# Splitting a weight slot in two halves: a four-layer transformer stack on one core

## The reference, cut to what matters

```python
def second_block(x, c, ada_w, ...):            # layers 3 and 4; layers 1 and 2 are built alike
    c_act = jax.nn.silu(c)
    for l in range(DEPTH):
        mod = (c_act @ ada_w[l] + ada_b[l])[:, None, :]
        sh_m, sc_m, gt_m, sh_f, sc_f, gt_f = jnp.split(mod, 6, axis=-1)
        h = rms_norm_2(x, norm_mix[l]) * (1 + sc_m) + sh_m
        y = hybrid_mixer(h, ...) if l % 2 == 0 else retention_mixer(h, ...)
        x = x + gt_m * y
        h = rms_norm_2(x, norm_ffn[l]) * (1 + sc_f) + sh_f
        x = x + gt_f * swiglu(h, ffn_w_in[l], ffn_w_out[l])
    return x
```

## Time and profile before

| | |
|---|---|
| median of 3 runs | 1724.1 us (1721.39 to 1725.34) |
| the profiled execution | 1721.6 us, span 1719.8 us |
| mean granted TensorE clock | 0.921 of full speed |
| TensorE matmuls busy | 1539.8 us, 90% of the span |
| VectorE, ScalarE, GpSimd busy | 1064.8, 719.7, 281.2 us |
| idle time of TensorE, total | 180 us |
| HBM read | 333.8 MB, 195 GB/s over the span |

### The profile page before, as it was taken

How to read it: one execution, slowest core, us unless ns; L and a number is a source line. 1 busy time by engine, 2 the same in 40 slices (tenths; PEclk the granted TensorE clock), 3 DMA queues, 4 the chain that set the end, 5 groups by cost and what they waited for, 6 DMA issues and landing times. The chain is left out here.

```text
span 1719.8 us, 27368 instructions
## 1 busy us (share of the span) xinstructions
PE 1539.8 (90%) x11950; PEld 1495.1 (87%) x11950; DVE 1064.8 (62%) x1278; ACT 719.7 (42%) x803; POOL 281.2 (16%) x221
## 2 busy tenths in 40 slices
PE   2888689999798779999999787999999998999999
PEld 2887579999788679999899686999999996989998
DVE  6776568688545447778675654667547763455544
ACT  2533345533553344543377432443334443343332
POOL 0000101044000012024200112000126900300012
PEclk7998579999799778999899997899999999989999
DMA  9660258888342045988544001477645772436560
GB/s 396 239 247 24 109 219 314 338 300 325 114 154 98 13 159 183 338 308 322 220 148 172 25 1 68 169 300 274 244 172 221 272 275 90 172 123 240 202 220 26
DMA packets 47207, 336.64 MB, mean 196 GB/s; under 512 B 5360, under 2 KB 5744, under 8 KB 6768
## 3 DMA queue, kind: packets, MB, share of 16 engines
q1 hardware_dynamic: 46224, 333.03, 51.9%
q10 hardware_dynamic: 864, 1.87, 0.3%
HBM read 333.83 MB, written 1.05 MB: 195 GB/s over the span
## 5 line engine op out<-in xcount | busy, mean ns | idle before, releaser
L420 DVE TENSOR_TENSOR weights_hi_lo<-ring,weights_hi_lo 128x2048 fp32r<-128x2048 f32 x213 | 512.2, 2406 | 397.5 <-ACT weights_hi_lo L414 396.3
L414 ACT ACTIVATE weights_hi_lo<-ring 128x2048 fp32r<-128x2048 f32 x213 | 407.6, 1915 | 630.0 <-PE PS L522 345.6
L522 PE MATMUL PS<-hi,weights_hi_lo 128*128 128x256 f32 x3200 | 526.9, 288 | 26.0 <-DVE weights_hi_lo L420 17.6
L522 PEld LDWEIGHTS PS<-hi,weights_hi_lo 128*128 128x128 f32 x3200 | 451.5, 196 | 29.8 <-DVE weights_hi_lo L420 19.5
L792 PE MATMUL PS<-acts_hi_lo,weights_hi_lo 128*128 128x256 f32 x3552 | 438.6, 286 | 29.4 <-DVE weights_hi_lo L420 16.3
L792 PEld LDWEIGHTS PS<-acts_hi_lo,weights_hi_lo 128*128 128x128 f32 x3552 | 432.3, 193 | 36.0 <-DVE weights_hi_lo L420 19.9
L522 PE MATMUL PS<-lo,weights_hi_lo 128*128 128x256 f32 x1600 | 327.0, 286 | 0.0
L522 PEld LDWEIGHTS PS<-lo,weights_hi_lo 128*128 128x128 f32 x1600 | 253.7, 195 | 0.0
L431 DVE CUSTOM_DVE_ANT_0 ring<-ring,cond 128x1024 f32<-128x1024 f32 x192 | 247.0, 1325 | 1.0 <-DMA smallS<-in_small_dram 0.9
L740 POOL CAST acts_hi_lo<-arena 128x512 fp32r<-128x512 f32 x74 | 67.1, 907 | 977.8 <-PE PS L792 544.7
L522 PE MATMUL PS<-weights_hi_lo,hi 128*128 128x256 f32 x1248 | 204.4, 286 | 10.1 <-DVE weights_hi_lo L420 8.9
(11 more groups left out here) (339 smaller groups left out, 1091.4 us busy)
## 6 DMA issues: line engine op xcount, KB each, us to landing
ring<-in_stream_dram SPq DMA_DIRECT2D x313, 1024.0 KB, 4.9
constS<-in_const_dram SPq DMA_DIRECT2D x1, 1856.0 KB, 11.4
cond<-in_rows_dram SPq DMA_DIRECT2D x2, 512.0 KB, 5.9
arena<-in_x_dram ACTq DMA_DIRECT2D x1, 1024.0 KB, 12.5
smallS<-in_small_dram SPq DMA_DIRECT2D x1, 883.0 KB, 12.7
out_dram<-arena ACTq DMA_DIRECT2D x2, 256.0 KB, 2.4
out_dram<-arena SPq DMA_DIRECT2D x2, 256.0 KB, 2.8
constS<-in_const_dram SPq DMA_DIRECT2D x1, 320.0 KB, 13.5
```

The source lines that it names most:

```text
L414: act.activation(wsp[:, g % 2, 0, :], ring[:, n % RING, :], ACT.Copy).then_inc(*hi_ready.one())
L420: dve.tensor_tensor(wsp[:, g % 2, 1, :], ring[:, n % RING, :], wsp[:, g % 2, 0, :].bitcast(F32), ALU.subtract).then_inc(used["dve"], 1)
L522: mm = pe.matmul(o, lhs, rhs, start=k + g + j == 0, stop=k == KD - 1 and j == 2, skip_group_check=True)
```

## The change

1. `split_hi`, `split_lo`: each slot is split by two operations of 1024 columns. The first half of a buffer may be written when TensorE has finished the first half of slot g - 2 (new semaphore `half_multiplied`), the second as before. VectorE signals the first half by `half_lo_ready`, the second by `used["dve"]`.
2. Column products wait for the first half before k = 0 and for the second before k = 4.
3. Row products go over all k with g = 0 and then over all k with g = 1, waiting for the second half of weights and activations in between; the last slot keeps the old order and waits for both halves first. `split_acts` works on one tile at a time and waits for one tile at a time (`state["mixed"]` now has an entry for each).
4. The norm's parts on ScalarE and VectorE are in two functions each, squares and root, and scaling. In `start_phase` ScalarE does squares and root ahead of the first slot's split, and VectorE the reciprocal ahead of its last modulation slot. ScalarE issues positions, constants and small inputs before it waits for the condition row.

```diff
 CW = SLOT // KD
+HALF = SLOT // 2
...
         multiplied, hi_ready = sig("slot_multiplied"), sig("hi_ready")
+        half_multiplied, half_hi_ready, half_lo_ready = sig("half_slot_multiplied"), sig("half_hi_ready"), sig("half_lo_ready")
         acts_hi, acts_lo = sig("acts_hi_ready"), sig("acts_lo_ready")
         def close():
...
             g = product_no[n]
-            if g >= 2:
-
-                act.wait_ge(multiplied.sem, g - 1)
-            act.activation(wsp[:, g % 2, 0, :], ring[:, n % RING, :], ACT.Copy).then_inc(*hi_ready.one())
+            for half, at, released, ready in ((0, 0, half_multiplied, half_hi_ready), (1, HALF, multiplied, hi_ready)):
+                if g >= 2:
+
+                    act.wait_ge(released.sem, g - 1)
+                act.activation(wsp[:, g % 2, 0, at:at + HALF], ring[:, n % RING, at:at + HALF], ACT.Copy).then_inc(*ready.one())
         def split_lo(dve, n):
             g = product_no[n]
-            dve.wait_ge(hi_ready.sem, g + 1)
-            dve.tensor_tensor(wsp[:, g % 2, 1, :], ring[:, n % RING, :], wsp[:, g % 2, 0, :].bitcast(F32),
-                              ALU.subtract).then_inc(used["dve"], 1)
+            for half, at, ready, done in ((0, 0, half_hi_ready, (half_lo_ready.sem, 1)), (1, HALF, hi_ready, (used["dve"], 1))):
+                dve.wait_ge(ready.sem, g + 1)
+                dve.tensor_tensor(wsp[:, g % 2, 1, at:at + HALF], ring[:, n % RING, at:at + HALF],
+                                  wsp[:, g % 2, 0, at:at + HALF].bitcast(F32), ALU.subtract).then_inc(*done)
         def mod_sums(dve, order, n, q, kk):
...
             def _(pe):
...
                 for i, n in enumerate(gemm):
-
-                    pe.wait_ge(used["dve"], ordinal[n][1])
                     if i >= banks:
...
                     for k in range(KD):
+                        if k == 0:
+                            pe.wait_ge(half_lo_ready.sem, product_no[n] + 1)
+                        if k == KD // 2:
+                            mm.then_inc(*half_multiplied.one())
+                            pe.wait_ge(used["dve"], ordinal[n][1])
                         for j, (w, h) in enumerate(pieces(w_hi, w_lo, hi, lo)):
...
-            def act_part(act):
+            def act_root(act):
                 for u, tiles in enumerate(UNITS):
...
                 act.activation(r, PS[:, 0, 0:TT], ACT.Sqrt, bias=cst("eps"), scale=1.0 / D).then_inc(*xrt.one())
+
+            def act_scale(act):
                 for k in range(KD):
...
-            def dve_part(dve):
+            def dve_root(dve):
                 dve.wait_ge(*xrt.at(1))
                 dve.reciprocal(r, r).then_inc(*xr.one())
+
+            def dve_scale(dve):
                 dve.wait_ge(*rx.at(1))
...
-            return pe_part, act_part, dve_part
+            return pe_part, (act_root, act_scale), (dve_root, dve_scale)
         def start_phase(blk):
...
             def _(act):
+                act.dma_start(posI[:, :], pos_in).then_inc(*inp.dma())
                 act.dma_start(constS[:, 0:EARLY_CONST], const[:, 0:EARLY_CONST]).then_inc(*inp.dma())
-                act.dma_start(posI[:, :], pos_in).then_inc(*inp.dma())
+                act.dma_start(smallS[:, 0:early_small], small[:, 0:early_small]).then_inc(*biases.dma())
                 act.wait_ge(*cond_in.at(16))
-                act.dma_start(smallS[:, 0:early_small], small[:, 0:early_small]).then_inc(*biases.dma())
                 act.dma_start(raw, x_in).then_inc(*x_in_sig.dma())
...
                         "p (k t) -> p k t", t=SEQ), ACT.Copy).then_inc(*xt.one())
+                norm[1][0](act)
                 for n in following:
                     split_hi(act, n)
-                norm[1](act)
+                norm[1][1](act)
...
             def _(pe):
...
                 dve.wait_ge(*biases.at(16))
-                for _, n, q, kk in todo:
+                for i, (_, n, q, kk) in enumerate(todo):
                     mod_sums(dve, order, n, q, kk)
+                    if i == len(todo) - 2:
+                        norm[2][0](dve)
                 for n in following:
                     split_lo(dve, n)
-                norm[2](dve)
+                norm[2][1](dve)
             close()
         def split_acts(pool, lhs, slots, before=0, ready=None):
...
                 a = rows_no[n]
-                if ready:
-                    pool.wait_ge(*ready[i])
-                if a >= 2:
-
-                    pool.wait_ge(multiplied.sem, product_no[rows_slots[a - 2]] + 1)
-                src = lhs[:, 2 * i:2 * i + 2, :]
-                pool.tensor_copy(asp[:, a % 2, 0, :, :], src).then_inc(*acts_hi.one())
-                pool.wait_ge(acts_hi.sem, a + 1)
-                pool.tensor_tensor(asp[:, a % 2, 1, :, :], src, asp[:, a % 2, 0, :, :].bitcast(F32),
-                                   ALU.subtract).then_inc(*acts_lo.one())
+                for g, released in enumerate((half_multiplied, multiplied)):
+                    if ready:
+                        pool.wait_ge(*ready[2 * i + g])
+                    if a >= 2:
+
+                        pool.wait_ge(released.sem, product_no[rows_slots[a - 2]] + 1)
+                    src = lhs[:, 2 * i + g, :]
+                    pool.tensor_copy(asp[:, a % 2, 0, g, :], src).then_inc(*acts_hi.one())
+                    pool.wait_ge(acts_hi.sem, 2 * a + g + 1)
+                    pool.tensor_tensor(asp[:, a % 2, 1, g, :], src, asp[:, a % 2, 0, g, :].bitcast(F32),
+                                       ALU.subtract).then_inc(*acts_lo.one())
         def rows_gemm_phase(blk, name, l, lhs, half, acts_split=0, acts_ready=None, next_norm=None):
...
             def _(pe):
                 for i, n in enumerate(slots):
-
-                    pe.wait_ge(used["dve"], ordinal[n][1])
                     w_hi, w_lo = halves_of(n, "rows")
                     a = rows_no[n]
-                    pe.wait_ge(acts_lo.sem, a + 1)
+                    pe.wait_ge(acts_lo.sem, 2 * a + (2 if i == last else 1))
                     a_hi, a_lo = asp[:, a % 2, 0, :, :], asp[:, a % 2, 1, :, :]
-                    for k in range(KD):
-                        if before and i == 0 and k == KD - 1:
+                    pe.wait_ge(half_lo_ready.sem, product_no[n] + 1)
+                    if i == last:
+
+                        pe.wait_ge(used["dve"], ordinal[n][1])
+                    for g, k in sorted(((g, k) for g in range(2) for k in range(KD)), key=lambda o: o[::-1] if i == last else o):
+                        if before and i + g == 0 and k == KD - 1:
...
                                 pe.wait_ge(*t)
-                        for g in range(2):
-                            for j, (w, x) in enumerate(pieces(w_hi, w_lo, a_hi, a_lo)):
-                                mm = pe.matmul(y_of(k), w[:, g, k * P:(k + 1) * P], x[:, g, :],
-                                               start=i + g + j == 0 and (k % 2 == 0 or k == KD - 1),
-                                               stop=i == last and g == 1 and j == 2, skip_group_check=True)
-                        if i == last and k in unit_ends:
+                        if i < last and g == 1 and k == 0:
+                            mm.then_inc(*half_multiplied.one())
+                            pe.wait_ge(used["dve"], ordinal[n][1])
+                            pe.wait_ge(acts_lo.sem, 2 * a + 2)
+                        for j, (w, x) in enumerate(pieces(w_hi, w_lo, a_hi, a_lo)):
+                            mm = pe.matmul(y_of(k), w[:, g, k * P:(k + 1) * P], x[:, g, :],
+                                           start=i + g + j == 0 and (k % 2 == 0 or k == KD - 1),
+                                           stop=i == last and g == 1 and j == 2, skip_group_check=True)
+                        if i == last and g == 0 and k == KD - 1:
+                            mm.then_inc(*half_multiplied.one())
+                        if i == last and g == 1 and k in unit_ends:
                             if k < KD - 1:
...
                     act.activation(r, PS[:, 0, 0:TT], ACT.Sqrt, bias=cst("eps"), scale=1.0 / D).then_inc(*yrt.one())
-                if norm:
-                    norm[1](act)
+                for part in norm[1] if norm else ():
+                    part(act)
...
             def _(dve):
...
                     ins.then_inc(*xu.one())
-                if norm:
-                    norm[2](dve)
+                for part in norm[2] if norm else ():
+                    part(dve)
             state["x_ready"] = [xu.at(u + 1) for u, tiles in enumerate(UNITS) for _ in tiles]
...
                 gemm_phase(blk, ("up", l), lambda i: 0, evac, split_next=U)
-                acts_ready = state["taken"]
+                acts_ready = [t for t in state["taken"] for _ in range(2)]
             else:
                 swiglu_phase(blk, l, U, tmp)
-                acts_ready = state["taken"][1::2]
+                acts_ready = [t for t in state["taken"][1::2] for _ in range(2)]
```

(2 more changed lines are left out.)

## The result

| | before | changed |
|---|---|---|
| median of 4 runs (lowest to highest) | 1722.7 us (1719.0 to 1725.3) | 1680.5 us (1678.4 to 1684.7) |
| profiled execution, span | 1721.6, 1719.8 us | 1681.1, 1679.4 us |
| mean granted clock | 0.921 | 0.926 |

The changed kernel takes 0.9759 of the time before (95% interval 0.9732 to 0.9787). The forecast was 1689 us within 1674 to 1706. The median became 42.3 us shorter and the profiled execution 40.5 us, against the sum of 35.1.

A forecast was written before the change was run, and what follows sets the result against it. The prediction took TensorE, busy 90% of the span, as the bound, with 180 us idle or slow to win from. Terms 6.3 + 10.0 + 2.0 + 7.7 + 4.0 + 6.1 - 1.0 = 35.1 gave 1686.5 profiled, 1689 median, range 1674 to 1706.

The forecast's parts named there:

- more is won: Rival: wait at 91.59 shrinks, all four clock drops go, two down projections win 2 to 3 us each; 1679 us, chance 0.12.
- wait at 91.59: First layer's projection: TensorE's 3.87 us wait, VectorE hardly paused since 82; claimed to move with its work and stay.
- The start: Start phase: squares and root ahead of the first split, so scaling begins at 35.5 instead of 41.80; 6.3 us won.
- Second slots: Second slot after a norm, eight phases: seven waits vanish, 10.0 us won, and 2.0 come off another.
- The eighth: Second slot at 469.54, ScalarE late behind another activation: 2.0 of its 3.68 us wait come off.
- Waits inside the projections: Seven waits of column products for low halves, 12.8 us, in three layers' projections: 7.7 us won.
- Clock: Granted-clock drops after four waits (52.4, 469.5, 498.8, 1529.9): three go, 4.0 us won, bounds zero and 7.
- Row products' first slots: First slot of row products: 3.8 us won in layers three and four, 2.3 in one and two, together 6.1.
- Row products with sums: 28 sums in first output product and first two down projections: extra turns and larger slack cancel, 0, bounds +3 and -11.
- the rival by which each extra pair of turns costs 2.2 us a slot: VectorE and GpSimd turns in 28 slots with sums: 62 us on top, kernel slower by 26, 1750 us, chance 0.02.
- Costs: One more operation a slot on ScalarE (0.1 us) and VectorE (0.15), mostly hidden, nine places on the path: -1.0 us.

The follow-up runs named there:

- halves alone: The changed kernel with the old order in the start phase (VectorE's, ScalarE's and the DMA order put back): 1687.0 us, 0.9804 of the kernel before.
- sums behind: The changed kernel with all modulation sums of the first output projection put behind its products: 1673.7 us, 0.9727 of the kernel before.
- whole activations: The changed kernel, but GpSimd splits activations two tiles per operation again and gives and takes whole buffers: 1679.7 us, 0.976 of the kernel before.
- the repeat: The changed kernel once more, unaltered, on another chip: 1678.6 us, 0.9784 of the kernel before.
- given back whole: The changed kernel, but buffers are released only after the whole slot, halves still made ready one by one: 1680.5 us, 0.9766 of the kernel before.
- Quarter operations: The changed kernel with each half of a weight slot written by two operations of 512 columns on ScalarE and VectorE: 1687.6 us, 0.9809 of the kernel before.
- sums earlier: The changed kernel with two modulation slots of the first projection moved to the front of its fifth product slot: 1672.5 us, 0.9713 of the kernel before.
- Start alone: The kernel before with only the change's start part (squares, root and reciprocal earlier, ScalarE's issues reordered): 1708.6 us, ratio 0.9938.

## Why the prediction was right, point by point

The median lies 8.5 us under the forecast of 1689: 5.4 us because more was won than the sum's 35.1, and 3.1 because the forecast set the median 2.5 us above the profiled execution and it came out 0.6 below. The time is nearer to the rival "more is won" (1679), and two of its three marks came: all four clock drops went and each of the two down projections won 2 to 3 us. The third, a shorter wait at 91.59, did not.

**The start (6.3 counted, 7.3 us came).** The order of events was the predicted one, with a smaller chain. The root was ready at 27.13 + 0.26 = 27.4, not at 30.4. Squares began at 20.97 instead of the 22.3 assumed, since x did not only land "no later" but sooner: TensorE's first work on it starts at 16.83 instead of 17.98 (at 15.7 to 17.1 in every kernel with the new order of issues, at 17.96 in "halves alone" with the old). And from the first to the last of TensorE's sums of squares it took 5.36 us instead of 6.99. So VectorE never waited for the root, and the about 1 us of waiting in the sum was not there.

**Second slots (10.0 and 2.0).** All seven waits are gone, the full 10.0. The eighth went from 3.68 to 1.82, 1.9 us.

**Waits inside the projections (7.7).** The pair in the first layer (2.03 and 3.87) and the 1.47 and 1.02 beside it, 8.4 us, became 1.15 + 3.97 = 5.1, 3.3 off where 3.9 was counted: 1.47 and 1.02 went whole, and 2.03 became 1.15. In the second layer 1.39 + 2.04 became 1.08 + 1.14, 1.2 off where 2.8 was counted; the third layer's 0.95 is gone. Together 5.4. That the wait at 91.59 "moves with its work and stays" was right to a tenth (3.97 us). The second layer is where this term was mis-sized. Counted by slots, its 1.39 went whole and its 2.04 became 1.08, but a new wait of 1.14 us stands ahead of the next slot, where there had been none. There VectorE's queue decides: ScalarE began that slot's hi at 480.12, and VectorE, busy with the mixers' work, its low half only at 482.81.

**Clock (4.0, bounds 0 to 7).** Windows of the kernel before behind three of the four waits (469.5, 498.8 and 1529.9; the fourth is in the earlier trace rows), and of the changed kernel behind the slots that answer to 52.4, 469.5 and 498.8 (us of PE, PEld, DVE, ACT, POOL with instructions; then granted clock, DMA share, GB/s):

```profile
469.60:473.10 3.50, 3.50 (x17) 3.50 (x18) 2.09 (x1) 0.04 (x1) 0.00 (x0) 0.53 0.66 234
498.80:502.30 3.50, 3.49 (x21) 3.49 (x22) 3.36 (x10) 1.98 (x2) 0.00 (x0) 0.70 0.67 232
1529.90:1533.30 3.40, 3.40 (x20) 3.40 (x21) 2.29 (x1) 2.02 (x3) 0.00 (x0) 0.66 0.68 236
```

```profile
43.70:46.70 3.00, 3.00 (x28) 3.00 (x27) 3.00 (x6) 1.80 (x4) 0.00 (x0) 1.00 0.97 397
451.96:455.46 3.50, 3.50 (x29) 3.50 (x30) 3.35 (x3) 2.49 (x5) 0.00 (x0) 1.00 0.41 82
477.00:480.50 3.50, 3.47 (x29) 3.50 (x30) 3.40 (x8) 0.97 (x3) 0.00 (x0) 1.00 0.38 101
```

The granted clock stays at 1.00 (2.4 GHz) where it had read 0.51 to 0.70, even behind the 1.82 us that remain at 451.96; it reads 1.00 at the second slot of the last layer's up product too (1490.9 to 1494.3), the place that answers to 1529.9. Where full speed has 30 matmuls in 3.5 us, 17 and 21 came; with nine missing at 1529.9 and eight at 52.4 that is 39 matmuls or 4.6 us. All four drops went, not three. The long one behind the wait of 91.59 shrank too:

```profile
91.60:98.60 7.00, 7.00 (x37) 7.00 (x38) 6.08 (x9) 4.00 (x4) 0.00 (x0) 0.58 0.80 294
```

```profile
79.00:86.00 7.00, 7.00 (x49) 7.00 (x49) 6.66 (x11) 3.99 (x5) 0.00 (x0) 0.81 0.80 301
```

In the seven us behind it come 49 matmuls instead of 37: 12 x 0.118 = 1.4 us. Together 6.0 where 4.0 had been counted. Why that stretch ended sooner no run isolated.

**Row products' first slots (6.1).** In layers three and four 6.07 and 5.80 us became 4.13 and 3.86: 1.94 each, counted 1.9; from ScalarE's start at 1025.40 to the product at 1028.10 it is 2.70, against 4.65. In layers one and two, waits of 6.38 and 6.39 became 5.24 and 5.25: 1.14 each where 1.5 had been counted, inside the bounds given (0.7 to 1.5), because GpSimd's cast and subtraction of one tile took 0.59 and 0.78 us and not half of 0.80 and 1.31. In layer one even this is given back at the last slot, where 0.8 was counted as kept: its wait grew from 2.68 to 3.63 us. From the first product to the last slot's it was 227.05 - 204.7 = 22.4 us before and 212.19 - 188.83 = 23.4 after: TensorE began earlier and met the same queue of VectorE. In "sums behind" the wait is gone with the sums, and whole activations leave it at 3.65. Beyond the wait, the last slot's first 24 matmuls took 5.46 us here and 4.31 to 4.60 in most of the other kernels with halves (4.63 before), at a granted clock of 0.50. The whole phase took 50.6 us against 48.9 in the repeat, and TensorE was busy in it for 41.4 against 39.1 us with the same matmuls: that difference is the clock's.

**Row products with sums (0, bounds +3 and -11).** This is the term that was mis-sized most: put at nothing, it measured 4.8. From the first product of the down projection to its norm it took 98.2 us in both layers before and 95.9 and 95.7 after, 4.8 us won (and the rival of more won had named 2 to 3 us each). The timeline of VectorE shows the slot's period there, against the earlier trace rows:

```profile
350.32 1.76 DVE L435 CUSTOM_DVE_ANT_0 ring<-ring,cond 128x1024 f32<-128x1024 f32 x1
352.43 1.59 POOL L757 TENSOR_TENSOR acts_hi_lo<-arena,acts_hi_lo 128x256 fp32r<-128x256 f32 x1
353.35 3.09 DVE L424 TENSOR_TENSOR weights_hi_lo<-ring,weights_hi_lo 128x1024 fp32r<-128x1024 f32 x2
356.36 1.76 DVE L435 CUSTOM_DVE_ANT_0 ring<-ring,cond 128x1024 f32<-128x1024 f32 x1
364.18 1.21 DVE L431 CUSTOM_DVE_ANT_0 ring<-ring,cond 128x1024 f32<-128x1024 f32 x1
```

The last row is the kernel before, one slot behind the sum at 358.20. 356.36 - 350.32 = 6.04 us, where the kernel before took 364.18 - 358.20 = 5.98 (the forecast's 358.20 to 364.26 ran to the end of the low half). Twice as many turns of half the length cost 0.06 us a slot: two low halves take 3.09 us against one of 3.37, while the sums and GpSimd's operations beside them take longer. That refutes the rival by which each extra pair of turns costs 2.2 us a slot. VectorE's period is still above TensorE's 5.7 us, but it no longer reaches TensorE: the first down projection's slots, from first product to first product, took up to 6.39 us before (five of the first 15 took 5.94 or more) and 5.68 to 5.76 after, but for the last but one with 5.98. The slots without sums and the larger slack take the rest up.

**Costs (-1.0).** Hidden, as said, though the operations cost more than was counted. Back to back, the pair of halves is 2.36 us of VectorE against 2.29 and 2.00 of ScalarE against 1.90. But in a running phase the second half waits for a signal of its own, and each half then takes its full 1.23 and 1.06 us. Over the kernel, 213 more operations made VectorE busy for 42.0 us more and ScalarE for 38.0, 0.20 and 0.18 us each, where the forecast had 0.15 and 0.1. In "given back whole", where ScalarE may write both halves at once, it is busy for 739.2 us, 19.5 more than before or 92 ns each. "Quarter operations" shows that the cover was near its end: the next doubling costs about 7 us of the time.

**The sum.** 7.3 (start) + 11.9 (second slots) + 5.4 (inside the projections) + 6.0 (clock) + 3.9 + 2.3 - 0.9 (row starts, and the last slot of the first layer) + 4.8 (slots with sums) = 40.7; the 40.5 us measured leave nothing visible for the cost of 1.0. The agreement is closer than the terms are known, and so partly luck: the first output projection became 2.7 us longer and only 0.9 of that is in the sum, and a repeat of the changed kernel had a span of 1676.5 us, 2.9 us away.

## What to carry to other kernels

When a buffer goes through two engines before a third, look at when its first use is possible, not only at buffers and shares of busy time: letting the consumer start on the first half was worth 21 of 42 us here, giving the buffer back by halves nothing measurable. Stop splitting where the producer's own queue is nearly full; there the order of the side work in that queue is the next thing to change (8 to 10 us for moves that add no instruction), phase by phase, since work moved ahead of another phase can cost there what it wins here. And price a short wait of TensorE with the slow stretch that can follow it.

## What the runs showed of the hardware

**The same phase differs by 6.7 us from kernel to kernel.** The sparse attention's phases have 233 matmuls with pauses between them, and in the twelve profiled kernels they took 56.2 to 62.9 us. Windows over such a phase, of the changed kernel and then of "sums earlier":

```profile
127.30:188.80 61.50, 42.98 (x233) 34.58 (x233) 29.73 (x66) 25.78 (x61) 2.30 (x4) 0.67 0.13 52
```

```profile
124.10:180.20 56.10, 37.20 (x233) 30.60 (x233) 29.71 (x66) 25.61 (x61) 2.25 (x4) 0.72 0.15 57
```

VectorE's busy time is equal within 0.02 us; TensorE's is 5.8 us apart and the granted clock reads 0.67 and 0.72. Both are far from 1.00: TensorE pauses often here, and the slow stretches fall in other places. Two executions of one program are 61.5 and 61.1 us in the first layer but 56.3 and 59.6 in the second. Outside these two phases no phase of those two executions differs by more than 1.7 us. "Start alone" owes 4.8 us of its profiled gain to this, so effects of a few us were read from single phases.

**Half the columns are not half the time on GpSimd.** Its groups in the kernel before:

```profile
L742 POOL TENSOR_TENSOR acts_hi_lo<-arena,acts_hi_lo 128x512 fp32r<-128x512 f32 x74 | 122.2, 1651 | 5.9
L740 POOL CAST acts_hi_lo<-arena 128x512 fp32r<-128x512 f32 x74 | 67.1, 907 | 977.8 <-PE PS L792 544.7 <-DVE arena L1478 113.4 <-DVE arena L897 92.7
```

After, the cast has 256 columns and takes 900 ns instead of 907, the subtraction 1198 instead of 1651. GpSimd's busy time rose from 281.2 to 397.8 us; it is hidden but for the row starts. Most of the rise is time shared with VectorE: in the third layer's down projection, where the two mostly miss each other, the median cast went from 0.61 to 0.40 us and the subtraction from 1.29 to 0.74. The time of one depends on what VectorE does: at 1025.33, with VectorE idle, the cast of 256 columns took 0.40 us, at 187.32 beside VectorE's scaling 0.59, and beside modulation sums or low halves 1.40.

**GpSimd's time goes with the length of VectorE's operations.** Two subtractions of "quarter operations", the first beside sums of 1024 columns, the second beside low quarters of 512:

```profile
343.38 1.60 POOL L760 TENSOR_TENSOR acts_hi_lo<-arena,acts_hi_lo 128x256 fp32r<-128x256 f32 x1
346.42 1.06 POOL L760 TENSOR_TENSOR acts_hi_lo<-arena,acts_hi_lo 128x256 fp32r<-128x256 f32 x1
```

The second is 0.54 us shorter, and VectorE's operation on 512 columns is 0.55 us shorter than the one on 1024 (0.68 against 1.23). So finer operations of VectorE give GpSimd time back: with GpSimd's own work unchanged, its busy time fell from 397.8 to 320.2 us. That fits the doubled turns that cost next to nothing above; no run isolated it further.
